# Six more seven-product groups in the up-projections of a two-layer trunk, and later loads behind the activation combinations

## The reference, cut to what matters

```
def swiglu(h, w_gate, w_up, w_down):
    return (jax.nn.silu(h @ w_gate) * (h @ w_up)) @ w_down
...
x = x + swiglu(rms_norm(x, ffn_norm[l]), w_gate[l], w_up[l], w_down[l])
```

## Time and profile before

| | us |
|---|---|
| median of 3 runs | 1756.67 |
| profiled execution | 1754.98 |
| its span, first to last instruction | 1753.2 |
| TensorE matmuls busy | 1737.7 (99%) |
| weight loads of TensorE busy | 1575.3 (90%) |
| VectorE busy | 1339.0 (76%) |
| ScalarE busy | 984.1 (56%) |
| GpSimd busy | 167.9 (10%) |

### The profile page before, as it was taken

The page is one execution under the profiler, slowest core; times in us unless marked ns, Lnnn a source line. Parts: engine busy times, 40 slices in busy tenths (PEclk is TensorE's granted clock), DMA queues, the critical chain, the costliest instruction groups (busy, mean ns, idle before and its releaser), DMA issues. The chain is left out here.

```text
span 1753.2 us, 29444 instructions
## 1 busy us (share of the span) xinstructions
PE 1737.7 (99%) x11142; PEld 1575.3 (90%) x11142; DVE 1339.0 (76%) x1772; ACT 984.1 (56%) x1336; POOL 167.9 (10%) x196
## 2 busy tenths in 40 slices
PE   9999999999999999999999999999999999999998
PEld 6889988999889999889999888898899998899987
DVE  5888766788667886788997778886578876788765
ACT  6656543566435665466775455664346653466543
POOL 2100000000000000224112420000000000000000
PEclk9999999999999999999999999999999999999999
DMA  6668765786767876665445456867568866688762
GB/s 226 216 209 246 220 205 179 240 252 188 242 196 206 244 245 210 198 204 157 150 138 170 154 170 226 240 180 254 191 197 242 251 208 200 207 249 247 225 213 92
DMA packets 103937, 363.24 MB, mean 207 GB/s; under 512 B 11664, under 2 KB 13072, under 8 KB 103696
## 3 DMA queue, kind: packets, MB, share of 16 engines
q1 hardware_dynamic: 94320, 327.03, 54.3%
q0 software_dynamic: 9216, 33.56, 11.1%
q10 hardware_dynamic: 288, 1.11, 0.2%
HBM read 326.01 MB, written 2.10 MB: 187 GB/s over the span
## 5 line engine op out<-in xcount | busy, mean ns | idle before, releaser
L1592 DVE TENSOR_TENSOR w_lo<-raw,w_hi 128x1024 fp32r<-128x1024 f32 (+1 forms) x720 | 857.8, 1200 | 267.1 <-ACT w_hi L1146 260.9
L1146 ACT ACTIVATE w_hi<-raw 128x1024 fp32r<-128x1024 f32 (+1 forms) x721 | 740.2, 1034 | 482.5 <-PE ps L635 388.5
L634 PE MATMUL ps<-xg,w_hi 128*128 128x512 f32 x1856 | 653.6, 392 | 6.7 <-DVE w_lo L1592 6.4
L635 PE MATMUL ps<-xg,w_lo 128*128 128x256 f32 x1856 | 522.9, 282 | 0.0
L634 PE MATMUL ps<-act,w_hi 128*128 128x512 f32 x1352 | 469.2, 390 | 0.0
L634 PEld LDWEIGHTS ps<-xg,w_hi 128*128 128x128 f32 x1856 | 348.4, 188 | 79.0 <-DVE w_lo L1592 9.2
L635 PE MATMUL ps<-act,w_lo 128*128 128x256 f32 x1352 | 381.3, 282 | 0.0
L635 PEld LDWEIGHTS ps<-xg,w_lo 128*128 128x128 f32 x1856 | 350.4, 189 | 0.0
L634 PEld LDWEIGHTS ps<-act,w_hi 128*128 128x128 f32 x1352 | 253.8, 188 | 53.1
L635 PEld LDWEIGHTS ps<-act,w_lo 128*128 128x128 f32 x1352 | 255.5, 189 | 0.0
L2212 POOL DMA_DIRECT2D raw<-raw x64 | 55.2, 863 | 1137.4 <-DVE raw L1672 986.5
(11 more groups left out here) (232 smaller groups left out, 1960.6 us busy)
## 6 DMA issues: line engine op xcount, KB each, us to landing
raw<-w_plain SPq DMA_DIRECT2D x224, 512.0 KB, 4.7
raw<-w_group SPq DMA_DIRECT2D x128, 512.0 KB, 5.5
raw<-w_down_rest SPq DMA_DIRECT2D x120, 448.0 KB, 4.1
raw<-raw POOLq DMA_DIRECT2D x64, 512.0 KB, 5.8
raw<-w_down_first SPq DMA_DIRECT2D x64, 512.0 KB, 3.7
raw<-w_o SPq DMA_DIRECT2D x32, 512.0 KB, 3.5
raw<-w_q_a SPq DMA_DIRECT2D x8, 512.0 KB, 4.1
raw<-w_kv_a SPq DMA_DIRECT2D x8, 512.0 KB, 4.0
```

What stands on the lines that cost most here:

```text
L634: pe.matmul(ps[:, bank, :], w_hi[:, s, j * P:(j + 1) * P], moving, start=start, stop=False)
L635: return pe.matmul(ps[:, bank, 0:SEQ], w_lo[:, s, j * P:(j + 1) * P], moving[:, 0:SEQ], start=False, stop=stop)
L1146: nc.scalar.activation(dst, src, ACT.Copy).then_inc(hi_ready, 1)
L1592: nc.vector.tensor_tensor(lo, src, hi.bitcast(F32), ALU.subtract).then_inc(lo_ready, 1)
```

## The change: what it does

- `PASS_GROUPS` goes from (2, 3, 3, 2, 3, 3) to (3, 4, 4, 3, 4, 4): 22 groups instead of 16, and 44 plain tiles instead of 56. The rest of the constants stay, so the mixed part of a layer's first pass has 42 group chunks with 9 plain ones (it had 28 with 17), that of each other pass 56 with 13 (it had 42 with 21).
- W22 and W21 of a layer's first group get the place after step 22 in SP's order (MIX_STEPS + SPLIT_SLOTS), where they had 19.
- TensorE waits for the copy of P5's result before P2, and for the sum over P2's result before P3; before, P3 waited for the copy of P5's and P2 for nothing of its own.

```
-PASS_GROUPS = (2, 3, 3, 2, 3, 3)
+PASS_GROUPS = (3, 4, 4, 3, 4, 4)
...
-                    free = CHUNK[UPS[q]] + MIX_STEPS + 1
+                    free = CHUNK[UPS[q]] + MIX_STEPS + SPLIT_SLOTS
...
                     elif r == "P7":
                         pe.wait_ge(part_copied, 3 * g + 3)
+                    elif r == "P2":
+                        pe.wait_ge(part_copied, 3 * g + 2)
                     elif r == "P3":
-                        pe.wait_ge(part_copied, 3 * g + 2)
+                        pe.wait_ge(part_summed, 3 * g + 1)
```

## The result

| | before | after |
|---|---|---|
| median of 6 runs each, us | 1755.65 | 1762.28 |
| lowest to highest | 1754.60 to 1757.03 | 1761.86 to 1764.41 |
| profiled execution, its span | 1754.98, 1753.2 | 1761.94, 1760.1 |

The ratio is 1.004 with a 95% interval of 1.0028 to 1.0051: slower by 5 to 9 us, and by more than the 0.2% that can be told from no change. The time lay inside the wide range of the prediction, 1743 to 1769 us, and just outside the 1748 to 1762 us of its own forecast; but the forecast of 1755.5 us was a gain, and the kernel became slower.

What follows compares the result with a forecast made beforehand. The prediction took TensorE's own stream, busy 99%, as the bound. From 1755.0 us, - 10.8 - 5.6 + 13.2 + 2 gave 1753.8 us for the profiled execution, 1755.5 us as median; own range 1748 to 1762, wide range 1743 to 1769.

Steps and rivals of the forecast that it cites:

- six groups: Up stretches: each added group saves TensorE 1.8 us against the two plain tiles it replaces, 10.8 us in all.
- later loads: Passes 0 and 3: plain chunk 23 no longer late behind W22 and W21 quarters, gain 5.6 us, bounds 0 to 7.6.
- the lead: First groups of passes 0 and 3: VectorE's backlog from P1 and P5 additions still leaves about 1.0 us a layer.
- starts of passes 1, 2, 4, 5: First groups of these passes: the prediction has no loss there.
- waits at the transposes: Between groups: TensorE waits for VectorE's fourth part_times ahead of the transposes, 13.2 us together.
- chain through W11: Split of P2, addition by DMA, then load of new W11 for P1b: 2 us, between 0 and 16 x 3.
- rival D: W11 chain decides: second addition and load make P1b late by 1 to 2 us at 16 places, 1767 us; chance 0.12.
- TensorE's new waits: Ahead of P2 and P3: cost nothing, at most 0.3 us in the few places without a plain chunk between.
- The walk to the transposes: VectorE's work followed to the transposes: waits of 1.5, 0.8, 0.5 us between groups; 0.5 and 0.5 in passes 0, 3.
- Rival B: VectorE arrives early at the transposes and only the gains stay: 1740 us, up to 1748; chance 0.20.
- Rival C: VectorE bounds the mixed stretches because its waits for ScalarE don't vanish: 1764 us, up to 1780; chance 0.20.
- Rival E: VectorE's successive instructions take their full recorded times, 1.22 us, so 31.0 us a group against TensorE's 29.4: 1775 us; chance 0.04.

Runs made afterwards that it cites:

- x_short: The changed kernel with each VectorE addition cut from 1024 columns to 128, kept behind the split by a wait: 1734.93 us, ratio 0.9887.
- x_loads: The kernel before, 16 groups, with only the later place of W22 and W21 in a layer's first pass: 1745.63 us, ratio 0.9949.
- x_waits: The kernel before with only TensorE's new waits ahead of P2 and P3: 1755.80 us, ratio 1.0007.
- x_times: The changed kernel with the fourth part_times one step sooner in VectorE's list, at P4b's own step: 1757.27 us, ratio 1.0013.
- x_spread3: The changed kernel with the edits of x_times and x_order, and mixed plain chunks put behind P3b, P4b and P1a of each group: 1756.39 us, ratio 1.0008.
- x_tail: The changed kernel with the edits of x_times and x_order, and a tail of 4 plain chunks instead of 7: 1781.12 us, ratio 1.015.
- x_shift: x_tail with the mixed plain chunks two places further on, so that plain tiles end elsewhere: 1763.61 us, ratio 1.0047.
- x_order: The changed kernel with the first group's quarter loads issued later in passes 1, 2, 4 and 5: 1758.36 us, ratio 1.002.
- x_mid: The changed kernel with (2, 4, 4, 2, 4, 4) groups, so groups added in passes 1, 2, 4 and 5 alone: 1761.73 us, ratio 1.0041.

## Why the prediction was wrong

| term | forecast, us | found | from |
|---|---|---|---|
| six groups | -10.8 | -11.2 | stretches of `x_short` and `x_loads` |
| later loads, net of what the lead still waits | -5.6 | -6.3 | -9.0 (`x_loads`), +2.7 (after, 1.08 and 0.27 a layer) |
| starts of passes 1, 2, 4, 5 | 0 | +6.2 | after, TensorE from start to start (1.0 of it is saved again in the first row) |
| waits at the transposes | +13.2 | +15.7 | the same, 16 places |
| chain through W11 | +2 | 0 | at most 0.2 us in one place, counted in the row above (rival D below) |
| TensorE's new waits | 0 | 0 | `x_waits`, `x_short` |
| waits under 0.25 us each | not counted | +2.9 | 27.5 in all, less the three above |
| outside the up stretches | 0 | -0.4 | the table of stretches |
| sum | -1.2 | +6.9 | the two profiled executions |

- **The step that failed** is a silent one in the sum: the prediction walked the lead of passes 0 and 3, and took the starts of passes 1, 2, 4 and 5 at nothing. They cost 6.2 us. There P1 and P5 also stand together now (0.7 us a pass), and in passes 1 and 2 plain chunk 3 comes late (2.1 and 1.3 us more). `PASS_GROUPS` feeds `up_loads` through `wanted_by`, which puts an eighth quarter ahead of that chunk, and it shifts the chunk number at which each pass begins, and with it the time at which SP gets past the first quarter. Both had to be worked out for every pass, not only where the diff names a place. Without this term the forecast would have been off by 1.9 us, but that is luck in part: the other terms miss by +2.5, +2.9, -0.4, -0.7, -2.0 and -0.4 us, and these nearly cancel.
- **The walk to the transposes** was right in place, releaser and pattern: 1.5, 0.8 and 0.5 us forecast, 1.73, 1.01 and 0.55 measured; for passes 0 and 3, 0.5 and 0.5 against 0.41 and 0.74. It is 2.5 us short in all. It also explains less than I thought: taking the fourth `part_times` out of the way (`x_times`) brought 5.0 of the 15.7 us, and the rest is work that VectorE has too much between two plain chunks. The third place is not at the transposes themselves but at the plain chunk just ahead of them.
- **The later loads** were undersized by themselves (9.0 against 5.6), but the net in after is close. The prediction added up the idle times of the rows, 3.8 us a layer; from start to start the same four places lose 4.5 us, and three restarts another 0.3. And it left 1.0 us where 0.25 us stayed. In the denser list the old place costs 14.4 us, since four quarters stand ahead of the chunk, and since the delay grows until the clock falls.
- **Rival B** (it fits) fell: `x_short` at 1734.9 shows what it would have given. **Rival C** held in a local form: not the mean of a stretch binds, but runs of 9 us without a gap. **Rival D** shows its sign twice in after, at the fourth group of passes 1 and 5, but hardly costs anything: ScalarE waits 0.45 and 1.89 us for a quarter of W11, and the third place of pass 5 loses 0.75 us where the other passes lose 0.55:
```profile
1618.57 1.06 ACT L1148 ACTIVATE w_hi<-raw 128x1024 fp32r<-128x1024 f32 x1 [1.89 <-DMA raw<-w_group]
```
  `x_spread3` shows a relative of it. **Rival E** falls by the same timeline: 1.13 to 1.14 us from start to start where the records say 1.22 us.
- The comparison that decides: each added group shortens a stretch without waits by 1.69 to 2.2 us and costs more in waits, so the whole change is a gain of 9.1 us (the loads) and a loss of 16.7 us (the groups).

That the additions of VectorE are the cause of the waits is shown (`x_short`), and that the places of the plain chunks among them matter is shown (`x_tail`, `x_shift`), and so is the part of the late load (`x_order`). Why the load is late in passes 1 and 2 alone is read from the planner and borne out by `x_mid`; no run changed only the chunk number at which a pass begins. Whether a list of 22 groups exists whose stretches stay at 148.65 us was not tried; the best up stretches were 150.94 us.

## What to carry to other kernels

Where several engines walk one list, room on the mean (95% busy here) says little: add up the follower's work over each run between two places where it can catch up, and do so at every kind of start and end, not only in the steady part. A count that a planner reads changes the order of loads far from the line edited, so write the issue order out before and after, pass by pass, and with it the condition that each load waits for: here two passes with the same order had their loads at different times. And time each part of a change alone: here one line of it was worth 9.1 us, and the larger part took 16.7 away.

## What the hardware showed that I had not expected

- After a wait of 3.98 us TensorE ran at half its rate: pairs of 0.64 against 0.35 us, at a granted clock of 0.50 from 1101.30 to 1105.80 us, which is its lower level, 1.2 GHz; over 1115 to 1130 us it is back at 1.00. The chunk took 5.3 us (1100.51 to 1105.80) instead of 2.77. Behind the waits of up to 1.6 us in after the mean clock stayed 0.999. The stall of 4 us is so paid nearly twice: the stretch is 168.5 us against after's 161.4.
- A load of 512 KB issued behind eight others landed after 10.4 us (301.47 to 311.83), where such loads took 5.5 us in the middle; the nine, issued within 4.8 us, landed 3.4 to 10.4 us after their issues, each later than the one ahead. ScalarE and VectorE then came so late that the first group began with 2.8 us of waits, with a lead of only four chunks to make up for it.
